# A three-block transformer stack on one core: the distance table's load moved behind a meeting, first latent parts in front of it, attention heads in another order

## The chip, the cores and the metric

The kernel runs on one NeuronCore of one Trainium2 chip. A core has five engines that run side by side and meet only at semaphores: TensorE (PE in the profile; PEld is its weight load), VectorE (DVE), ScalarE (ACT), GpSimd (POOL) and SyncE (SP), which here only starts transfers. The metric is the time of one execution on the device in microseconds (us), lower is better. All arithmetic is float32; TensorE multiplies float32 values that have been split into a rounded high part and a remainder (low part).

## The reference

One token sequence of 512 tokens with 1024 features goes through a first block, and then through a second block with two layers. The change touches only the mixing part of those two layers:

```python
for l in range(DEPTH_2):                                   # two layers
    x = x + 0.5 * swiglu(rms_norm(x, ffn1_norm[l]), ...)
    h = rms_norm(x, mix_norm[l])
    pa, pb, pc, pd = jnp.split(h @ w_in[l], IN_SPLITS, axis=-1)
    ya = neighbourhood_mixer(pa, ...)      # 4 near heads: q reads 8 rows x 32 columns of keys, plus a bias
    yb = mla_mixer(pb, ...)                # 4 latent heads: 96 wide, 512 keys
    yc = diff_mixer(pc, ..., t5_bias, ...) # 4 differential heads: softmax of 2 maps each, bias by distance
    yd = gqa_mixer(pd, ...)                # 4 shared heads: 2 key heads, 512 keys
    x = x + jnp.concatenate([ya, yb, yc, yd], axis=-1) @ w_out[l]
    x = x + 0.5 * swiglu(rms_norm(x, ffn2_norm[l]), ...)
    x = rms_norm(x, final_norm[l])
```

The four mixers are independent of each other, so their heads can be computed in any order. Each head is softmax(q k + bias) v; the bias of the differential heads is a table by distance (t5_bias), that of the near heads a table by offset.

## The kernel before, in words

The program is a row of stages. Between stages stands a meeting (`handover`, L393): every engine drains its queue, says so on a semaphore, and waits until the others have said it. GpSimd's drain is L421. SyncE waits for the same four semaphores before the first transfers of the next stage.

Each of the two layers has a stage `mixer_inputs` and then a stage `mixers`. `mixer_inputs` multiplies the normalized input by 22 units of weights; at its end GpSimd waits for the last unit, and issues the transfer of the distance table (L2618, 1792 KB) into `hlo`, a buffer that TensorE reads until that last unit. Then comes the meeting.

`mixers` runs `attention` (L956) on 20 groups of 4 steps, 80 steps in all, one step for 128 queries of one head (or of one of the two maps of a differential head). Before the change the groups are: latent heads (steps 0 to 15), near heads (16 to 31), shared heads (32 to 47), differential heads (48 to 79). A step t is:

- TensorE, L985: scores(t), three products of 512 columns (latent, shared), three of 256 (near), or one of 512 (differential), into one of four banks
- VectorE, L1071 or, with a bias, L1078: the row minimum `low` (scores are kept with their sign turned)
- ScalarE, L1032: the exponential, `prob`
- TensorE, L993: four (near: two) transposes of `prob`; ScalarE, L1039: copy to `probT`
- TensorE, L1004: product with the values `vB`, `vA`, `vD`, `vC` (latent, near, shared, differential)

TensorE's queue holds scores(t+4), the transposes of t, the values of t-2, in this order for t = 0, 1, 2 and so on; each waits in order. Scores are four steps ahead and have four banks, so scores(t+4) waits until the exponential (with a bias: the minimum) of step t is done.

The query side lives in two slots of four tiles in `hhi`, used in turn (`user` lists the first step of each user of a slot, `ends` the first step after it). VectorE fills them: `splits` (L2106) puts pieces of work at given steps t of its queue: `parts` writes high parts (a cast, L2111) and low parts (a subtraction, L2115). A piece that overwrites a slot first waits for `qk_done`, the count of score steps done, of the slot's user two before. Latent heads 0 and 1 are written at t = -1, the start of the stage. Key parts that several heads share go to `parted`, 8 tiles.

Near and shared queries fill 64 of 128 partitions. The other 64 are zeroed by GpSimd (L2081), once for each slot, after it has added the near heads' bias and mask (L2065, 12 additions, `nabias`), which in turn wait for SyncE's 9 loads (L2051, L2054).

The differential heads' slots are not written by VectorE. SyncE copies them from `parted` with 16 transfers of 64 KB for a head (L2101, L2104; "stack load" below), four such loads for u = 10 to 13, and before each it waits for `parted`, and for `qk_done` to reach `ends[u - 2]`.

Of the kernel before, what the change touches and what calls it, by code (L numbers as in the profile page):

```python
# [24 lines left out]
P = 128  # L25
# [2002 lines left out]
def mixers(k, mem, l, near, latent, diff, shared, parted, lam, ytok):  # L2028
# [11 lines left out]
    diff_parts = [apart[0:2] + apart[6:8], apart[2:6]]  # L2040
    user = list(range(0, 32, 4)) + list(range(32, 80, 8))
# [18 lines left out]
    def _(pool):  # L2060
        pool.wait_ge(*k.t5_landed.all())
        pool.wait_ge(*loaded)
        for h in range(4):
            for o in range(3):
                nc.gpsimd.tensor_tensor(bias[:, h, o, :].rearrange("p (r j) -> p r j", j=32),  # L2065
                                        wide[:, h, :, 16 - 8 * o:48 - 8 * o],
                                        mask[:, o, :].rearrange("p (r j) -> p r j", j=32), ALU.add)\
                    .then_inc(*k.na_ready.up())

# [14 lines left out]
    ready = {user[h]: [k.latent_split.at(h + 1)] for h in range(4)}  # L2084
    for v in range(4):
        ready[user[4 + v]] = [k.keys_split.at(1 + v // 2), zeroed[v % 2], k.padded.at(v + 1)]
    for v in range(2):
        ready[user[8 + v]] = [k.keys_split.at(3), k.padded.at(5 + v)]
# [19 lines left out]
    def splits(dve, t):  # L2108
# [27 lines left out]
        if t == -1:  # L2136
            latent_head(0)
# [4 lines left out]
        if t in (5, 9):  # L2142
            c = (t - 5) // 4
            parts([(kA[:, c, :], *near_keys[c])], k.keys_split)
        if t in (8, 12, 16, 20):
            h = (t - 8) // 4
            dve.wait_ge(*k.qk_done.at(ends[2 + h]))
            r = 64 * (h % 2)
            parts([(qA[r:r + 64, h // 2, :], slot[h % 2][0][r:r + 64], slot[h % 2][1][r:r + 64])], k.padded)
        if t == 13:  # L2150
            parts([(kD[:, :], *shared_keys)], k.keys_split)
        if t in (24, 28):
            v = (t - 24) // 4
            dve.wait_ge(*k.qk_done.at(ends[6 + v]))
# [3 lines left out]
        if t in (30, 48):  # L2158
            c = 0 if t == 30 else 1
# [7 lines left out]
    for h in range(4):  # L2167
# [4 lines left out]
                           out=ytok[:, :, GW + h * 64:GW + h * 64 + 64], add=False, factor=None))  # L2172
    for h in range(4):
# [9 lines left out]
    for v in range(2):  # L2183
        for j in range(2):
            h = 2 * v + j
            groups.append(dict(steps=[dict(pairs=three(slice(u * P, (u + 1) * P), *slot[v][2 * j:2 * j + 2], shared_keys),
                                           width=T, bias=None, values=[vD[:, t, v, :] for t in range(TB)])
                                      for u in range(TB)],
                               out=ytok[:, :, 3 * GW + h * 64:3 * GW + h * 64 + 64], add=False, factor=None))
# [10 lines left out]
    sums = {45: (1, bias[:, :, 0, :]), 47: (0, bias[:, :, 1, :]), 61: (6, bias[:, :, 2, :]), 68: (2, head(0)),  # L2200
            76: (3, head(1)), 82: (4, head(2))}

    def squares(act, t):
        if t in (44, 46, 60):
            i = (44, 46, 60).index(t)
            at, done = ((GW, 4), (0, 8), (3 * GW, 12))[i]
            act.wait_ge(*k.o_read.at(done))
            if i == 0:
                act.wait_ge(*k.low_done.at(32))
# [12 lines left out]
    attention(k, groups, mem, bias_ready=(4 * TB, na_ready), ready=ready, splits=splits, on_act=squares)  # L2222
# [33 lines left out]
def mixer_inputs(k, w, l, near, latent, diff, shared, lat_parts, lam, gain, sb):  # L2256
# [245 lines left out]
    def _(dve):  # L2502
# [7 lines left out]
        for s in range(2 * UNITS + 1):  # L2510
# [66 lines left out]
            if s in parts:  # L2577
# [5 lines left out]
                    .then_inc(*k.rn_ready.up())  # L2583
            if s == 40:
# [11 lines left out]
    def _(pool):  # L2596
# [16 lines left out]
        for r in range(8, 11):  # L2613
            cosine(r)
        t5 = k.hlo[:, 0:7, :].rearrange("p c t -> p (c t)").rearrange("p (h t) -> p h t", h=4)
        pool.wait_ge(k.units_done.sem, n0 + UNITS)
        pool.wait_ge(k.tables_out, 32)
        pool.dma_start(t5, bass.AP(k.t5_dram.tensor, 0, [[1, P], [1024, 4], [1, 896]]).bitcast(F32R))\  # L2618
            .then_inc(*k.t5_landed.up(by=16))
# [176 lines left out]
def build(nc, w, consts, out):  # L2796

    with ExitStack() as ctx:
# [22 lines left out]
        k.into_landed = signal("into_landed")  # L2821
# [115 lines left out]
```

## Time and profile before

| what | value |
|---|---|
| median of 3 runs | 3440.15 us (3438.2 to 3444.74) |
| profiled execution, its own time | 3431.85 us |
| its span | 3430.1 us |
| granted TensorE clock over the span, of 1 | 0.968 |
| PE, PEld, DVE, ACT, POOL busy | 97%, 78%, 51%, 38%, 6% |
| chain that ended last, by engine | PE 89%, DVE 6%, issue 2%, ACT 2% |
| `mixers` of the first layer, meeting to the last product with values | 1695.02 to 1861.89 us |
| `mixers` of the second layer, the same | 2832.95 to 2993.18 us |

A row of the timeline has: start in us, duration in us, engine, line, operation, out<-in, count, and in brackets the idle time of the engine just before it and what ended it. A row of the windows has: the stretch, its length, busy time of each engine with the number of instructions, the granted TensorE clock (1.00 is 2.4 GHz, 0.50 is 1.2 GHz), the mean busy share of the DMA engines and GB/s. Matmuls overlap, so the time that one takes from the next is read from start to start.

### The profile page before, as it was taken

The numbers are of one execution on the slowest core, as the hardware profiler recorded it, in microseconds if no ns is written. First come the engines' busy times: TensorE is split into PE (matmuls) and PEld (weight loads), VectorE is DVE, ScalarE is ACT, GpSimd is POOL, SyncE is SP. The second block draws the span as 40 slices with busy tenths as digits, with TensorE's granted clock in tenths as the row PEclk, the third lists the DMA queues.
The fourth block names the chain that finished last, engine by engine and source line by source line (L and its number), as shares of the span: only waits on it lengthen the run. The fifth ranks groups of instructions, "written<-read, shape, count | busy, mean of one in ns | idle before, by whom it ended". The sixth has DMA issues, their size and how long they took to land.

```text
span 3430.1 us, 41354 instructions
## 1 busy us (share of the span) xinstructions
PE 3320.0 (97%) x15399; PEld 2659.7 (78%) x15399; DVE 1764.3 (51%) x2614; ACT 1299.0 (38%) x1849; POOL 213.8 (6%) x234
## 2 busy tenths in 40 slices
PE   8979998999999999999899999999999998999998
PEld 6667876888888888875598888878887567878887
DVE  7354487445553455335646555445553565555532
ACT  4326655233332333223246333333322324643332
POOL 1001100000000000010200100010000011010000
PEclk9969999999999999999979999999999997999999
DMA  5310022333333333332202333333333321223332
GB/s 126 92 49 4 1 68 80 96 94 94 95 95 96 97 94 92 99 93 68 70 13 66 90 96 96 94 92 98 98 97 88 85 60 27 69 86 98 97 91 63
DMA packets 518249, 275.12 MB, mean 80 GB/s; under 512 B 39523, under 2 KB 510407, under 8 KB 517986
## 3 DMA queue, kind: packets, MB, share of 16 engines
q1 hardware_dynamic: 513154, 262.77, 27.6%
q0 software_dynamic: 3600, 9.85, 0.9%
q8 instruction: 89, 1.46, 0.2%
q10 hardware_dynamic: 1360, 0.66, 0.1%
q14 instruction: 46, 0.38, 0.0%
HBM read 262.70 MB, written 2.14 MB: 77 GB/s over the span
## 4 chain that ended last, share of the span: by engine, by line
PE 89%; DVE 6%; issue 2%; ACT 2%; POOLq 0%; POOL 0%; DMA 0%; DVEq 0%; ACTq 0%
PE bank L375 24%; PE bank L376 24%; PE bank L377 24%; PE bank L1004 5%; PE bank L985 5%; PE bank L993 3%; PE bank L2389 1%; DVE wlo L351 1%; PE bank L1688 1%; PE bank L2372 1%; POOLq L421 0%; PE bank L2359 0%; DVE xc L1894 0%; DVE q L932 0%; PE bank L690 0%
## 5 line engine op out<-in xcount | busy, mean ns | idle before, releaser
L375 PE MATMUL bank<-hhi,whi 128*128 128x512 f32 (+1 forms) x2504 | 992.6, 396 | 7.4 <-DVE wlo L351 5.1
L376 PE MATMUL bank<-hhi,wlo 128*128 128x512 f32 (+1 forms) x2504 | 977.2, 390 | 0.0
L377 PE MATMUL bank<-hlo,whi 128*128 128x512 f32 (+1 forms) x2504 | 977.1, 390 | 0.0
L351 DVE TENSOR_TENSOR wlo<-raw,whi 128x1024 fp32r<-128x1024 f32 x485 | 608.6, 1257 | 587.2 <-ACT whi L344 578.3
L344 ACT CAST whi<-raw 128x1024 fp32r<-128x1024 f32 x485 | 505.1, 1046 | 408.6 <-PE bank L377 394.9
L375 PEld LDWEIGHTS bank<-hhi,whi 128*128 128x128 f32 (+1 forms) x2504 | 470.4, 188 | 149.0 <-issue 45.1
L377 PEld LDWEIGHTS bank<-hlo,whi 128*128 128x128 f32 (+1 forms) x2504 | 470.4, 188 | 100.2
L376 PEld LDWEIGHTS bank<-hhi,wlo 128*128 128x128 f32 (+1 forms) x2504 | 470.8, 188 | 99.0 <-issue 3.4
L375 PE MATMUL bank<-uhi,whi 128*128 128x512 f32 x880 | 348.7, 396 | 0.0
L376 PE MATMUL bank<-uhi,wlo 128*128 128x512 f32 x880 | 348.2, 396 | 0.0
L377 PE MATMUL bank<-ulo,whi 128*128 128x512 f32 x880 | 348.2, 396 | 0.0
L594 ACT CAST uhi<-gate 128x512 f32 x110 | 68.2, 620 | 597.1 <-DVE gate L618 597.1
L611 DVE TENSOR_TENSOR up<-bank,rinv 128x512 f32<-128x512 f32 x110 | 76.0, 691 | 288.1 <-PE bank L377 288.1
L1039 ACT COPY probT<-bank 128x512 f32<-128x512 f32 (+3 forms) x288 | 140.5, 488 | 148.1 <-PE bank L993 147.0
L377 PEld LDWEIGHTS bank<-ulo,whi 128*128 128x128 f32 x880 | 165.4, 188 | 39.9
L375 PEld LDWEIGHTS bank<-uhi,whi 128*128 128x128 f32 x880 | 165.4, 188 | 39.8
L376 PEld LDWEIGHTS bank<-uhi,wlo 128*128 128x128 f32 x880 | 165.4, 188 | 39.4
L463 POOL TENSOR_TENSOR sq<-sq 128x512 f32<-128x512 f32 x49 | 63.8, 1302 | 1825.6 <-ACT sq L481 1825.6
L993 PEld LDWEIGHTS bank<-ident,prob 128*128 128x128 f32 x896 | 120.0, 149 | 46.8 <-issue 24.6
L993 PE MATMUL bank<-ident,prob 128*128 128x128 f32 x896 | 154.6, 286 | 0.9 <-ACT prob L1032 0.6
L621 DVE TENSOR_TENSOR ulo<-gate,uhi 128x512 f32 x110 | 76.2, 693 | 99.5 <-ACT uhi L594 99.5
L985 PE MATMUL bank<-kT,q 128*128 128x128 f32 (+3 forms) x256 | 98.1, 469 | 5.3 <-POOLq L421 5.3
(443 smaller groups left out, 3651.8 us busy)
## 6 DMA issues: line engine op xcount, KB each, us to landing
raw<-in_ffn_w_gate SPq DMA_DIRECT2D x88, 512.0 KB, 3.8
raw<-in_ffn_w_up SPq DMA_DIRECT2D x88, 512.0 KB, 3.7
raw<-in_w_in SPq DMA_DIRECT2D x78, 512.0 KB, 3.8
raw<-in_ffn_w_down SPq DMA_DIRECT2D x64, 512.0 KB, 4.0
raw<-in_w_out SPq DMA_DIRECT2D x24, 512.0 KB, 4.1
raw<-in_ffn_w_down SPq DMA_DIRECT2D x32, 384.0 KB, 3.4
raw<-in_w_gate SPq DMA_DIRECT2D x22, 512.0 KB, 3.9
raw<-in_w_up SPq DMA_DIRECT2D x22, 512.0 KB, 3.7
```

The lines of the kernel that those rows point to most:

```text
L344: k.nc.scalar.copy(k.whi[:, slot, :], k.raw[:, slot, :]).then_inc(k.hi_split.sem, 1)
L351: k.nc.vector.tensor_tensor(k.wlo[:, slot, :], k.raw[:, slot, :], k.whi[:, slot, :].bitcast(F32), ALU.subtract)\
L375: mm(out, whi, hi(kc), start=start and i == 0, stop=False)
L376: mm(out, wlo, hi(kc), start=False, stop=False)
L377: last = mm(out, whi, lo(kc), start=False, stop=stop and i == kcs - 1)
L594: nc.scalar.copy(uhi[:, bass.ds(i * 2 + e, 1), :], gate[:, e:e + 1, :])\
L611: nc.vector.tensor_tensor(up[:, e, :], bank[u + 1][:, :], k.rinv[:, :], ALU.mult)\
L621: nc.vector.tensor_tensor(ulo[:, bass.ds(i * 2 + e, 1), :], gate[:, e:e + 1, :], uhi[:, bass.ds(i * 2 + e, 1), :].bitcast(F32), ALU.subtract)\
L985: last = nc.tensor.matmul(score(t), q, key, start=i == 0, stop=i == len(pairs) - 1)
L993: last = nc.tensor.transpose(k.bank[4 + t % 2][:, b * P:b * P + P], prob[:, t % 2, b * P:b * P + P], k.ident[:, :])
L1004: last = nc.tensor.matmul(mixed(g)[:, e, :], probT[:, t % 3, b * P:b * P + P], v, start=b == 0, stop=b == len(values) - 1)
L1039: nc.scalar.copy(probT[:, v % 3, 0:width[v]], k.bank[4 + v % 2][:, 0:width[v]])\
```

## The change

Three things, in each of the two layers.

1. The load of the distance table leaves the end of `mixer_inputs`, and is the first thing that GpSimd does in `mixers`, behind the meeting. GpSimd waits for its landing after the 12 additions, no longer before them.
2. The parts of latent head 0 leave t = -1 of `attention`, and are computed by VectorE at the end of `mixer_inputs`, in front of the meeting.
3. The order of heads is latent (steps 0 to 15), shared (16 to 31), near (32 to 47), differential (48 to 79). `user`, the places in `parted`, the steps of the pieces in `splits` and of the sums of squares follow.

```diff
-    diff_parts = [apart[0:2] + apart[6:8], apart[2:6]]
-    user = list(range(0, 32, 4)) + list(range(32, 80, 8))
+    diff_parts = [apart[4:8], apart[0:4]]
+    user = [0, 4, 8, 12, 16, 24, 32, 36, 40, 44, 48, 56, 64, 72]
...
     def _(pool):
-        pool.wait_ge(*k.t5_landed.all())
+        distances = k.hlo[:, 0:7, :].rearrange("p c t -> p (c t)").rearrange("p (h t) -> p h t", h=4)
+        pool.wait_ge(k.tables_out, 32)
+        pool.dma_start(distances, bass.AP(k.t5_dram.tensor, 0, [[1, P], [1024, 4], [1, 896]]).bitcast(F32R))\
+            .then_inc(*k.t5_landed.up(by=16))
         pool.wait_ge(*loaded)
...
                     .then_inc(*k.na_ready.up())
+        pool.wait_ge(*k.t5_landed.all())
...
-    ready = {user[h]: [k.latent_split.at(h + 1)] for h in range(4)}
+    ready = {user[h]: [k.latent_split.at(h)] for h in range(1, 4)}
+    for v in range(2):
+        ready[user[4 + v]] = [k.keys_split.at(1), zeroed[v], k.padded.at(v + 1)]
     for v in range(4):
-        ready[user[4 + v]] = [k.keys_split.at(1 + v // 2), zeroed[v % 2], k.padded.at(v + 1)]
-    for v in range(2):
-        ready[user[8 + v]] = [k.keys_split.at(3), k.padded.at(5 + v)]
+        ready[user[6 + v]] = [k.keys_split.at(2 + v // 2), k.padded.at(3 + v)]
...
         if t == -1:
-            latent_head(0)
             latent_head(1)
...
-        if t in (5, 9):
-            c = (t - 5) // 4
-            parts([(kA[:, c, :], *near_keys[c])], k.keys_split)
-        if t in (8, 12, 16, 20):
-            h = (t - 8) // 4
-            dve.wait_ge(*k.qk_done.at(ends[2 + h]))
-            r = 64 * (h % 2)
-            parts([(qA[r:r + 64, h // 2, :], slot[h % 2][0][r:r + 64], slot[h % 2][1][r:r + 64])], k.padded)
-        if t == 13:
+        if t == 5:
             parts([(kD[:, :], *shared_keys)], k.keys_split)
-        if t in (24, 28):
-            v = (t - 24) // 4
-            dve.wait_ge(*k.qk_done.at(ends[6 + v]))
+        if t in (8, 12):
+            v = (t - 8) // 4
+            dve.wait_ge(*k.qk_done.at(ends[2 + v]))
             r = 64 * v
             parts([(qD[r:r + 64, j, :], slot[v][2 * j][r:r + 64], slot[v][2 * j + 1][r:r + 64]) for j in range(2)],
                   k.padded)
-        if t in (30, 48):
-            c = 0 if t == 30 else 1
+        if t in (14, 18):
+            c = (t - 14) // 4
+            parts([(kA[:, c, :], *near_keys[c])], k.keys_split)
+        if t in (20, 28, 32, 36):
+            h = (20, 28, 32, 36).index(t)
+            dve.wait_ge(*k.qk_done.at(ends[4 + h]))
+            r = 64 * (h % 2)
+            parts([(qA[r:r + 64, h // 2, :], slot[h % 2][0][r:r + 64], slot[h % 2][1][r:r + 64])], k.padded)
+        if t in (34, 48):
+            c = 0 if t == 34 else 1
...
-        if t in (44, 46, 60):
+        if t in (50, 52, 60):
...
+            if s == 2 * UNITS:
+                for x, to in ((qB, 0), (kB, 2)):
+                    nc.vector.tensor_copy(k.hhi[0:MD, to, :], x[0:MD, 0, :]).then_inc(*k.latent_hi.up())
+                for i, (x, to) in enumerate(((qB, 0), (kB, 2))):
+                    dve.wait_ge(*k.latent_hi.at(i + 1))
+                    nc.vector.tensor_tensor(k.hhi[0:MD, to + 1, :], x[0:MD, 0, :], k.hhi[0:MD, to, :].bitcast(F32),
+                                            ALU.subtract)
...
-        t5 = k.hlo[:, 0:7, :].rearrange("p c t -> p (c t)").rearrange("p (h t) -> p h t", h=4)
-        pool.wait_ge(k.units_done.sem, n0 + UNITS)
-        pool.wait_ge(k.tables_out, 32)
-        pool.dma_start(t5, bass.AP(k.t5_dram.tensor, 0, [[1, P], [1024, 4], [1, 896]]).bitcast(F32R))\
-            .then_inc(*k.t5_landed.up(by=16))
```

On GpSimd, around the meeting of the first layer (L419 ends the old stage, L2059 begins the new one; `ytok` holds the near table while it is added):

```order
-L2618 DMA hlo<-t_by_distance 128x4x896 [waits tables_out,units_done]
...
 L419 UNCONDITIONAL_BRANCH
 L2059 UNCONDITIONAL_BRANCH [waits dve_finished,act_finished,pe_finished]
-L2065 TENSOR_TENSOR nabias<-ytok 128x256 [waits offsets_landed,t5_landed]
-L2065 TENSOR_TENSOR nabias<-ytok 128x256 x11
-L2073 UNCONDITIONAL_BRANCH
-L2081 MEMSET hhi 64x2048 [waits qk_done,na_ready]
-L2081 MEMSET hhi 64x2048 [waits slot_zeroed,qk_done]
+L2063 DMA hlo<-t_by_distance 128x4x896 [waits tables_out]
+L2068 TENSOR_TENSOR nabias<-ytok 128x256 [waits offsets_landed]
+L2068 TENSOR_TENSOR nabias<-ytok 128x256 x11
+L2077 UNCONDITIONAL_BRANCH [waits t5_landed]
+L2085 MEMSET hhi 64x2048 [waits qk_done,na_ready]
+L2085 MEMSET hhi 64x2048 [waits slot_zeroed,qk_done]
```

The load has moved past the meeting, and the wait for it past the 12 additions; the two memsets still stand behind the additions.

On VectorE, the start of `mixers` before (L1044 is its first instruction behind the meeting):

```order
1013 L2593 TENSOR_SCALAR lam<-lam 128x1 [waits lam_dot]
1014 L413 UNCONDITIONAL_BRANCH
1015 L1044 UNCONDITIONAL_BRANCH [waits pool_finished,act_finished,pe_finished]
1016 L2111 CAST hhi<-qB 96x512
1017 L2111 CAST hhi<-kB 96x512
1018 L2115 TENSOR_TENSOR hhi<-qB,hhi 96x512 [waits part_hi]
1019 L2115 TENSOR_TENSOR hhi<-kB,hhi 96x512
1020 L2111 CAST hhi<-qB 96x512
```

and now, where after latent head 3 and the shared keys the shared queries `qD` of step 8 follow:

```order
1013 L2603 TENSOR_SCALAR lam<-lam 128x1 [waits lam_dot]
1014 L2589 CAST hhi<-qB 96x512
1015 L2589 CAST hhi<-kB 96x512
1016 L2592 TENSOR_TENSOR hhi<-qB,hhi 96x512 [waits latent_hi]
1017 L2592 TENSOR_TENSOR hhi<-kB,hhi 96x512 [waits latent_hi]
1018 L413 UNCONDITIONAL_BRANCH
1019 L1044 UNCONDITIONAL_BRANCH [waits pool_finished,act_finished,pe_finished]
1020 L2115 CAST hhi<-qB 96x512
...
1036 L2115 CAST parted<-kD 128x512
1037 L2119 TENSOR_TENSOR parted<-kD,parted 128x512 [waits part_hi]
1038 L1071 TENSOR_REDUCE low<-bank 128x1 [waits qk_done,exp_done] x3
1039 L2115 CAST hhi<-qD 64x512 [waits qk_done]
```

Four instructions have moved in front of the meeting, and the queries behind step 8 are the shared heads' four instructions instead of the near heads' two.

On TensorE, the last of near head 3 and the first differential step now (`stacked0` is the landing of the stack load into slot 0):

```order
5010 L985 MATMUL bank<-parted,hhi 128x256 [waits low_done]
5011 L985 MATMUL bank<-parted,hhi 128x256 x2
5012 L993 MATMUL bank<-ident,prob 128x128 [waits pt_copied,exp_done]
5013 L993 MATMUL bank<-ident,prob 128x128
5014 L1004 MATMUL bank<-vA,probT 128x65 [waits pt_copied]
5015 L1004 MATMUL bank<-vA,probT 128x65
5016 L985 MATMUL bank<-hhi 128x512 [waits stacked0,low_done]
5017 L993 MATMUL bank<-ident,prob 128x128 [waits pt_copied,exp_done]
```

Before, the steps ahead of that wait were those of the last shared head:

```order
5011 L985 MATMUL bank<-parted,hhi 128x512 [waits exp_done]
5012 L985 MATMUL bank<-parted,hhi 128x512 x2
5013 L993 MATMUL bank<-ident,prob 128x128 [waits pt_copied,exp_done]
5014 L993 MATMUL bank<-ident,prob 128x128 x3
5015 L1004 MATMUL bank<-vD,probT 128x65 [waits pt_copied]
5016 L1004 MATMUL bank<-vD,probT 128x65 x3
5017 L985 MATMUL bank<-hhi 128x512 [waits stacked0,exp_done]
```

The first differential scores now stand behind narrow near steps, where wide shared ones stood; by `ends[8]`, the stack load of slot 0 waits for `qk_done` = 44 (`user[9]`), where it waited for 40.

## Rows read from the trace of the kernel before

**Rows 1.** Windows: `mixers` of the first layer, from the meeting to the last values.
```profile
1695.02:1861.89 166.87, 157.62 (x1040) 145.29 (x1040) 90.08 (x221) 93.72 (x169) 16.30 (x17) 0.85 0.20 44
```

**Rows 2.** Timeline and chain that ended last: the meeting of the first layer.
```profile
1687.42 0.80 POOL L2618 DMA_DIRECT2D hlo<-t_by_distance  x1 [13.84 <-PE bank L377]
1687.40 7.62 POOLq L421
1688.68 0.15 DVE L2593 TENSOR_SCALAR lam<-lam 128x1 f32<-128x1 f32 x1
1695.35 0.42 DVE L2111 CAST hhi<-qB 96x512 fp32r<-96x512 f32 x1 [6.52 <-POOLq L421]
1697.49 5.84 PE L985 MATMUL bank<-hhi 96*128 96x512 f32 x15 [8.80 <-DVE hhi L2115]
```

**Rows 3.** Windows of TensorE alone: its stretches at either clock.
```profile
1697.49:1702.07 4.58, 4.58 (x11) 0.50 0.93 175
1715.76:1760.14 44.38, 44.38 (x193) 0.50 0.00 1
1760.14:1861.90 101.76, 98.44 (x775) 1.00 0.24 58
2852.40:2883.06 30.66, 30.57 (x122) 0.50 0.00 1
2883.06:2993.20 110.14, 106.80 (x849) 1.00 0.22 54
```

**Rows 4.** Timeline: GpSimd's additions, latent head 3's parts, TensorE's gap (second layer last).
```profile
1707.75 10.22 POOL L2065 TENSOR_TENSOR nabias<-ytok 128x256 f32<-128x256 f32 x12 [19.52 <-DMA ytok<-na_by_offset]
1709.23 0.91 DVE L2111 CAST hhi<-qB 96x512 fp32r<-96x512 f32 x1 [2.68 <-PE bank L985]
1712.07 1.20 DVE L2115 TENSOR_TENSOR hhi<-kB,hhi 96x512 fp32r<-96x512 f32 x1
1714.71 0.96 PE L985 MATMUL bank<-hhi 96*128 96x512 f32 x3 [2.19 <-ACT prob L1032]
2852.49 1.65 PE L985 MATMUL bank<-hhi 96*128 96x512 f32 x3 [1.74 <-ACT prob L1032]
```

**Rows 5.** Timeline: scores of neighbouring steps: latent, shared, near, differential, a pair each.
```profile
1721.52 1.63 PE L985 MATMUL bank<-hhi 96*128 96x512 f32 x3
1725.36 1.63 PE L985 MATMUL bank<-hhi 96*128 96x512 f32 x3
...
1787.85 0.94 PE L985 MATMUL bank<-parted,hhi 128*128 128x512 f32 x3
1789.88 0.95 PE L985 MATMUL bank<-parted,hhi 128*128 128x512 f32 x3
...
1760.58 0.61 PE L985 MATMUL bank<-parted,hhi 128*128 128x256 f32 x3
1761.61 0.61 PE L985 MATMUL bank<-parted,hhi 128*128 128x256 f32 x3
...
1816.88 0.49 PE L985 MATMUL bank<-hhi 128*128 128x512 f32 x1
1818.45 0.48 PE L985 MATMUL bank<-hhi 128*128 128x512 f32 x1
```

**Rows 6.** Windows: while only the distance table was moving.
```profile
1690.00:1694.00 4.00, 0.00 (x0) 0.00 (x0) 0.00 (x0) 0.00 (x0) 0.00 (x0) 0.73 1.08 384
```

**Rows 7.** SyncE's timeline: first load and last load of the first layer's stack loads.
```profile
1784.82 2.52 SPq L2101 DMA_DIRECT2D hhi<-parted  x4
...
1793.24 2.49 SPq L2104 DMA_DIRECT2D hhi<-parted  x4
...
1828.41 2.41 SPq L2101 DMA_DIRECT2D hhi<-parted  x4
...
1835.93 2.49 SPq L2104 DMA_DIRECT2D hhi<-parted  x4
```

**Rows 8.** By tile `parted`: from issue to landing, least, median, most.
```profile
DMA to landing us min/median/max: 1.9/2.0/3.3
```

More of the change, by code:

```diff
@@ L2172, in mixers @@
                            out=ytok[:, :, GW + h * 64:GW + h * 64 + 64], add=False, factor=None))
+    for v in range(2):
+        for j in range(2):
+            h = 2 * v + j
+            groups.append(dict(steps=[dict(pairs=three(slice(u * P, (u + 1) * P), *slot[v][2 * j:2 * j + 2], shared_keys),
+                                           width=T, bias=None, values=[vD[:, t, v, :] for t in range(TB)])
+                                      for u in range(TB)],
+                               out=ytok[:, :, 3 * GW + h * 64:3 * GW + h * 64 + 64], add=False, factor=None))
     for h in range(4):
@@ L2182, in mixers @@
         groups.append(dict(steps=heads, out=ytok[:, :, h * 64:h * 64 + 64], add=False, factor=None))
[L2183 to L2189, printed above, removed]
     for h in range(4):
@@ L2199, in mixers @@
     head = lambda h: bias[:, :, 0, h * HD:(h + 1) * HD]
-    sums = {45: (1, bias[:, :, 0, :]), 47: (0, bias[:, :, 1, :]), 61: (6, bias[:, :, 2, :]), 68: (2, head(0)),
+    sums = {51: (1, bias[:, :, 0, :]), 53: (6, bias[:, :, 1, :]), 61: (0, bias[:, :, 2, :]), 68: (2, head(0)),
             76: (3, head(1)), 82: (4, head(2))}
     def squares(act, t):
-        if t in (44, 46, 60):
-            i = (44, 46, 60).index(t)
-            at, done = ((GW, 4), (0, 8), (3 * GW, 12))[i]
+        if t in (50, 52, 60):
+            i = (50, 52, 60).index(t)
+            at, done = ((GW, 4), (3 * GW, 8), (0, 12))[i]
             act.wait_ge(*k.o_read.at(done))
             if i == 0:
-                act.wait_ge(*k.low_done.at(32))
+                act.wait_ge(*k.low_done.at(48))
             nc.scalar.activation(bias[:, :, i, :], ytok[:, :, at:at + GW], ACT.Square).then_inc(*k.y_sq.up())
@@ L2220, in squares @@
                                      bias=k.eps[:, 0:1]).then_inc(*k.y_root.up())
-    attention(k, groups, mem, bias_ready=(4 * TB, na_ready), ready=ready, splits=splits, on_act=squares)
+    attention(k, groups, mem, bias_ready=(8 * TB, na_ready), ready=ready, splits=splits, on_act=squares)
     @k.block.vector
@@ L2821, in build @@
         k.into_landed = signal("into_landed")
+        k.latent_hi = signal("latent_hi")
         k.x_odd, k.vt_copied, k.t5_landed = signal("x_odd"), signal("vt_copied"), signal("t5_landed")
```

## The prediction

> **What bounds the kernel now.** The page first: TensorE is busy 97% of the span and 89% of the chain that ended last, so only what makes TensorE wait, or run at the lower clock, can be won. The change lies in the two `mixers` stages, so the windows of these come next: in the first layer 166.9 us with TensorE busy for 157.6 of them, at a mean granted clock of 0.85 [rows 1]. So some 9 us of the stage are gaps, and more is lost to the clock. The timeline of the meeting shows the largest gap. GpSimd issues the distance table's load at 1687.42, and its drain ends 7.62 us later, about when the load has landed; VectorE waits 6.52 us for it, then splits latent head 0 for 2.14 us, and TensorE starts at 1697.49 after 8.80 us without work [rows 2]. The windows by clock come third. TensorE ran at 0.50 (1.2 GHz) right after the meeting, again from 1715.76 to 1760.14, and in the second layer from 2852.40 to 2883.06; the rest ran at 1.00 (2.4 GHz) [rows 3]. The timeline ahead of the two later falls shows why: VectorE is at latent head 3's parts, and TensorE has nothing for 2.19 us in the first layer, 1.74 in the second; during or just behind these the clock falls [rows 4]. It came back only after 44 and 31 us, though TensorE was busy throughout.
>
> What a step costs TensorE, start to start: latent at the lower clock 3.84 us; shared at the higher 2.03, near 1.03, differential 1.57 [rows 5]. A latent step has the same instructions as a shared one, so 2.03 for it too. The full clock would nearly halve both low stretches.
>
> **The start of the stage.** With the table's load behind the meeting, GpSimd drains at once. VectorE's last instruction in front of it ends at 1688.83; the four instructions for head 0 take 2.14 us there as they did behind it, to 1690.97 [rows 2]. Some 0.25 us for the meeting itself (the first cast started 0.33 after the drain's end) makes TensorE start at 1691.2 and not 1697.49: -6.3 us for each layer, -12.6 in all. What is late next: the parts of head 1, 2.1 us again, which hold the first minimum as before, so the pipeline starts shifted by the same amount. TensorE's gap at the meeting falls from 8.8 to about 2.5 us. The table's own landing has until step 48 to come.
>
> **The first seam: GpSimd's additions against VectorE's parts.** While GpSimd adds, head 3's parts take 4.04 us (1709.23 to 1713.27) and not the 2.1 that they take alone; a cast is 0.91 and not 0.42 [rows 4, 2]. TensorE has work for 3.3 us from 1709.23 (its gap of 2.19 ends at 1714.71), and minimum and exponential take 1.44 behind the parts: 4.04 + 1.44 - 3.3 is the gap. Alone, the parts would leave 0.3. GpSimd began 12.7 us behind the meeting. Now the table's 1792 KB share the DMA engines with the near tables; alone they moved at 384 GB/s [rows 6], so at most 4.7 us later: 17.4. Head 3's parts now come at about 10 to 12 us, in front of the additions. But the four instructions of step 8 (shared queries) stand at 18 to 20 us, right on them: 4.0 us and not 2.1. The steps around are of the same kind, so the gap is 2.2 us, as before but four steps later. So I expect the clock to fall again, at step 13. If the additions began 3 us later the gap would be gone. I take a low stretch of 14 us for each layer (before it was 31 and 44, never rose among latent steps and rose among those of the heads behind them, in the second layer at the first ones; now only three latent steps, 11.5 us, are left behind the gap). Lost before: half of 44.4 and 30.7, 37.5 us; lost now: half of 28, 14 us. Term: -23.5, between -37.5 (no fall) and +31 (low until the near heads at step 32: 19 steps that lose 1.81 each, 34 us a layer). The value is nearest to the row of the second layer, where the rise came with the first step of another kind.
>
> The Trainium skill has a rule for this seam (SBUF — State Buffer, "Who interferes with whom"): a VectorE instruction with two SBUF inputs or in a two-port mode and a GpSimd one exclude each other, and the later blocks until the earlier ends. By that rule each of the four would wait for up to one addition of 0.85 us (10.22 / 12), 3.4 in all; the rows have 1.9 in all, so the trace agrees that they hinder each other, and the price by rows is the lower. By the rule's 3.4 the gap would be 3.7 us, and the sum 3 us higher over both layers.
>
> GpSimd's memset for the first shared slot needs additions (10.2) and memset (1.9): 17.4 + 12.1 = 29.5 us, when step 16's scores are due at about 29 to 31. Cost 0 to 0.5; I take 0.
>
> **The second seam: the first stack load.** 16 transfers leave SyncE from 1784.82 to 1795.73, 10.9 us; the fastest of the first layer's four, 1828.41 to 1838.42, 10.0 us; landing 2.0 more [rows 7, 8]. So 12.0 to 12.9 us from the slot being free to step 48's scores. Before, it started when the scores of step 39 were done, and 8 shared steps of 2.03 (16.2 us) covered it. Now the slot's last user is near head 2: it starts after step 43, and ahead of step 48's scores TensorE has only four near steps (4.1) and one set of transposes and values (0.6): 4.7 us. It then waits 12.7 - 4.7 = 8.0 us, in each layer: +16, between +14.6 and +16.4. Nothing else can run there: transposes stand behind the scores in TensorE's queue. ScalarE's two squares of steps 50 and 52 and VectorE's sums, formerly over steps 44 to 47, fall just behind it, where the others have caught up, so cost nothing.
>
> Eight idle us are more than the gaps after which the clock fell, so it falls. How long it stays low among differential heads no row shows. Low, a differential step would be about 1.57 x 3.84 / 2.03 = 3.0 us, 1.4 more. The bounds are 0 and all 32 steps (+45 for a layer). I take some 8 steps (24 us at the low clock would lose 11; I shade to 12 us, since the first steps behind the wait have their work ready and TensorE has no gap): +6 for each, +12 in all. It is nearest to the restart behind the meeting, which was back at 1.00 after 4.6 us [rows 3], and far from the two long ones; that is the weakest term. At the low clock the second stack load (12 us) hides behind 8 steps; at the high one it would stick out by 1.7 us.
>
> **The near heads.** TensorE's gaps at the higher clock, 101.76 - 98.44 and 110.14 - 106.80, 3.3 us in each layer [rows 3], come from VectorE's pieces of work between near steps (near, shared and differential parts in one run of 16 short steps). Now half of these pieces stand in the wide latent and shared steps, where 3.3 us of TensorE's work cover 1.1 for a piece of two instructions and 1.4 for minimum and exponential: -2.5 for each, -5.
>
> **Sum.** -12.6 - 23.5 + 16 + 12 - 5 = -13. The restart behind the meeting is shorter and less likely at the low clock: -2.3 at best, I take -2. So -15 against the profiled execution's own 3431.85 (span 3430.1, 1.75 around it): 3417. The three runs lie 6 to 13 us above that execution. Its second layer had 14 us less at the low clock than its first, which is worth 7; runs with both stretches long are the usual ones, and the new order has less to lose there. So against the median of 3440.15 I take -20: 3420.
>
> **Rivals.**
>
> - *The clock holds, or is back at once.* If the additions miss step 8's parts and the fall at step 48 lasts only as after the meeting: -12.6 - 37.5 + 16 + 4 + 3.4 (second stack load in sight) - 5 - 2 = -34, some 3400 to 3406. For it: the additions' start is within 3 us of missing. Against: 8 us of idling are certain by the rows.
> - *Slower: the differential heads run at the low clock.* Place: step 48, where the stack load leaves TensorE idle. Price: 45 us a layer instead of 6. In both layers: -15 + 78 = +63, 3500; in one, or half the way in both: +20 to +25, 3460. It decides once the low stretch behind step 48 lasts over 27 us a layer. For it: before, a busy TensorE stayed low for 31 and 44 us [rows 3], and no row shows the clock rising among differential steps. Against: the clock did rise in the narrow steps of the near heads.
> - *Nothing left over.* The stall of 8 us and long low stretches (about 25 us at each of the two places) eat the start's gain: 3434 to 3446. What I call the low stretches' lengths is the only thing to change.
> - *The start is not won.* GpSimd's drain could be slow for another reason than the load. Then TensorE starts about 2 us earlier only, +8: 3428. Against: its 7.62 us go with the load's time. Small.
>
> **Chances.** Forecast (two short low stretches, or one long) 0.42; clock holds 0.18; slower 0.24, of which one layer 0.14; nothing left 0.13; start not won 0.03. A difference under 0.2% (7 us) can't be told from none. Faster: 0.42 + 0.18 + 0.03, less 0.03 for the forecast's upper edge: 0.60. Same: 0.13 and that edge: 0.15. Slower: 0.25. The forecast's own range is 3408 to 3431. The range for 8 in 10 leaves out the best of the clock's case and the two-layer loss: 3398 to 3456.
>
> **What would show it.** Timeline: TensorE starts 2 to 3 us after its last product in front of the meeting, with no 7.6 us drain. A gap of some 2 us before the scores of step 13 with VectorE's `qD` parts at twice their time, next to GpSimd's additions. A gap of 7 to 9 us in front of the first differential scores, put down to the DMA into `hhi`. Windows by clock: 0.50 behind each. I'd be wrong if that gap is under 4 us (the stack load is quicker, or near steps slower), or if the clock behind it is low for over 27 us or for none.

## The result, and the profile after

| what | before | after |
|---|---|---|
| median, in one comparison | 3438.2 us (5 runs) | 3416.69 us (5 runs, 3409.7 to 3420.75) |
| ratio of the two, 95% interval | | 0.994 (0.9924 to 0.9956) |
| profiled execution, its own time | 3431.85 us | 3416.69 us |
| last product in front of the meeting to last product with values, layer one / two | 173.2 / 166.6 us | 158.8 / 160.8 us |

The change makes the kernel 21.5 us, or 0.6%, faster; 3420 had been predicted, in a range of 3398 to 3456. Of the two traces the stages account for 14.4 and 5.8 us, 20.2 in all. TensorE comes 4.06 us later to the first meeting in the profiled execution of after (1692.75 where it was 1688.69), in a part that the change doesn't touch: in the first block its granted clock was 0.50 for 17.1 us from 242.06 on, where it had been for 6.8 us from 241.2 on. The other parts outside the two stages lose 1 us more, so the own times differ by only 15.2.

The timeline of the meeting in the kernel after, against [rows 2]:

```profile
1692.81 0.41 DVE L2589 CAST hhi<-qB 96x512 fp32r<-96x512 f32 x1
1694.08 0.68 DVE L2592 TENSOR_TENSOR hhi<-kB,hhi 96x512 fp32r<-96x512 f32 x1
1695.12 0.72 PE L985 MATMUL bank<-hhi 96*128 96x512 f32 x2 [2.37 <-DVEq L415]
1695.53 0.80 POOL L2063 DMA_DIRECT2D hlo<-t_by_distance  x1 [17.88 <-DVEq L415]
2819.19 1.22 PE L985 MATMUL bank<-hhi 96*128 96x512 f32 x2 [2.38 <-DVEq L415]
```

TensorE's gap of 8.80 is 2.37 and 2.38. The drain of 7.62 us is gone, and what is waited for now is VectorE's.

The timeline of the first seam after, against [rows 4]:

```profile
1712.34 9.54 POOL L2068 TENSOR_TENSOR nabias<-ytok 128x256 f32<-128x256 f32 x12 [16.00 <-DMA ytok<-na_by_offset]
1714.87 1.42 DVE L2115 CAST hhi<-qD 64x512 fp32r<-64x512 f32 x2 [3.03 <-PE bank L985]
1716.33 2.24 DVE L2119 TENSOR_TENSOR hhi<-qD,hhi 64x512 fp32r<-64x512 f32 x2
1719.26 0.69 ACT L1032 ACTIVATE prob<-bank,low 128x512 f32<-128x512 f32 x1 [3.31 <-DVE low L1071]
1720.00 1.65 PE L985 MATMUL bank<-hhi 96*128 96x512 f32 x3 [1.87 <-ACT prob L1032]
2845.35 0.97 PE L985 MATMUL bank<-hhi 96*128 96x512 f32 x3 [2.26 <-ACT prob L1032]
```

The additions begin 17.2 us behind the restart (TensorE's first product behind the meeting, at 1695.12), on top of the four pieces of `qD`. Those take 3.7 us (1714.87 to 1718.57), the minimum and the exponential follow late, and TensorE has nothing for 1.87 us. The windows of TensorE alone, against [rows 3]:

```profile
1696.14:1699.55 3.41, 3.41 (x9) 0.50 1.00 212
1719.90:1733.60 13.70, 13.60 (x51) 0.50 0.00 0
1733.70:1788.30 54.60, 52.07 (x411) 1.00 0.05 13
1792.85:1798.40 5.55, 5.55 (x22) 0.50 0.38 87
1798.60:1851.50 52.90, 51.63 (x427) 1.00 0.33 80
2846.40:2859.90 13.50, 13.50 (x58) 0.50 0.00 0
2919.22:2924.80 5.58, 5.58 (x22) 0.50 0.43 101
```

The long low stretches of 44.38 and 30.66 us have become 13.7 and 13.5, and two short ones are new. These lie behind the second seam; TensorE's timeline there, then SyncE's:

```profile
1785.27 0.56 PE L1004 MATMUL bank<-vA,probT 128*128 128x65 f32 x4
1792.85 0.77 PE L985 MATMUL bank<-hhi 128*128 128x512 f32 x1 [7.02 <-DMA hhi<-parted]
...
2919.22 0.76 PE L985 MATMUL bank<-hhi 128*128 128x512 f32 x1 [8.16 <-DMA hhi<-parted]
```

```profile
1781.20 2.52 SPq L2105 DMA_DIRECT2D hhi<-parted  x4
...
1788.82 2.49 SPq L2108 DMA_DIRECT2D hhi<-parted  x4
```

The stack load starts at 1781.20, and its landing lets TensorE go on 11.65 us later; TensorE has been out of work since 1785.83.

### The profile page after: what moved, and what is told of

Its sections match the earlier page's. It is cut to its first block, busy times and chain, and to the rows that moved or that the text cites. A ratio compares the mean times of both kernels' runs of the same rounds, so it can differ in the third digit from the quotient of the medians.

```text
span 3414.9 us, 41348 instructions
## 1 busy us (share of the span) xinstructions
PE 3306.4 (97%) x15399; PEld 2645.2 (77%) x15399; DVE 1762.5 (52%) x2614; ACT 1298.9 (38%) x1849; POOL 211.8 (6%) x234
## 3 DMA queue, kind: packets, MB, share of 16 engines
q8 instruction: 89, 1.46, 0.2%
## 4 chain that ended last, share of the span: by engine, by line
PE 90%; DVE 6%; ACT 2%; issue 1%; SPq 1%; DMA 0%; DVEq 0%; POOL 0%; ACTq 0%; POOLq 0%; PEldq 0%
PE bank L375 24%; PE bank L377 24%; PE bank L376 24%; PE bank L1004 5%; PE bank L985 5%; PE bank L993 3%; PE bank L2392 1%; DVE wlo L351 1%; PE bank L2375 1%; PE bank L1688 1%; PE bank L2362 1%; DVE xc L1894 0%; DVE q L932 0%; PE bank L690 0%; PE bank L1707 0%
```

## The experiments

Each difference between two kernels is taken from their ratios to the kernel before (in brackets behind each time, with the 95% interval), in us of 3440. A ratio's own interval is about 0.2% either way, so 7 us, and kernels that were compared together share the runs of the kernel before.

**The two halves of the change alone.** `start_only` is the kernel before, with the first two of the three things:

```diff
-        pool.wait_ge(*k.t5_landed.all())
...
+        pool.dma_start(distances, bass.AP(k.t5_dram.tensor, 0, [[1, P], [1024, 4], [1, 896]]).bitcast(F32R))\
...
+        pool.wait_ge(*k.t5_landed.all())
...
-            latent_head(0)
...
+            if s == 2 * UNITS:
+                for x, to in ((qB, 0), (kB, 2)):
```

> The kernel before, with only the start of the change: the distance table's load behind the meeting, latent head 0's parts in front of it; heads in the old order. Theory (each part of the change does what its rows say, and the parts add up): TensorE starts 6.4 us earlier behind both meetings, -12.8. GpSimd's additions move from 12.7 to about 17.4 us behind the meeting, past latent head 3's parts and onto the near heads' pieces, which have two instructions and not four; so the gap at step 7 goes, any later gap is under 1.5 us, and the long low stretches (half of 44 and 31 us lost) shrink or go: 3390 to 3412. Rival 1 (the start gains, but the clock falls as before, since the additions are not what makes the gap): 3425. Rival 2 (the drain is slow for another reason than the load): TensorE's first gap stays over 6 us, 3434.

3383.54 us (0.9853, 0.9831 to 0.9875): 51 us faster than before, better than the theory's 3390 to 3412, and 30 us faster than the whole change. Its timeline, and one window of the first layer:

```profile
1702.45 0.42 DVE L2115 CAST hhi<-qB 96x512 fp32r<-96x512 f32 x1 [2.68 <-PE bank L985]
1708.48 9.62 POOL L2068 TENSOR_TENSOR nabias<-ytok 128x256 f32<-128x256 f32 x12 [16.02 <-DMA ytok<-na_by_offset]
1711.02 0.54 DVE L2115 CAST hhi<-qA 64x512 fp32r<-64x512 f32 x1 [3.03 <-PE bank L985]
1711.59 1.11 DVE L2119 TENSOR_TENSOR hhi<-qA,hhi 64x512 fp32r<-64x512 f32 x1
```

```profile
1695.00:1833.10 138.10, 132.92 (x1031) 1.00 0.29 62
```

Latent head 3's parts begin at 1702.45, 6.0 us ahead of the additions; in [rows 4] they began 1.5 us behind their start. The additions now fall on pieces of two instructions (1.7 us for the first), which fit beside a latent step, and the clock stays at 1.00 from the end of the restart's low stretch (1695.46) to the end of the stage. 12.8 us of start and 37.5 us of clock make 50.3, and the two stages are 50.9 us shorter by the traces.

`order_only` has the third thing alone:

```diff
-        distances = k.hlo[:, 0:7, :].rearrange("p c t -> p (c t)").rearrange("p (h t) -> p h t", h=4)
...
+        pool.wait_ge(*k.t5_landed.all())
         pool.wait_ge(*loaded)
...
         if t == -1:
+            latent_head(0)
```

> The changed kernel with the old start: the table's load in front of the meeting and latent head 0's parts behind it, heads in the new order. Theory: 8.8 us without work at both meetings as before; the additions meet latent head 3's parts as before, gap of about 2 us at step 7, and a low stretch of 20 to 44 us in a layer; a wait of 7 to 8 us in front of step 48 with a low stretch of 5 to 7 us behind it, +21 for both layers. Against before: +21, less up to 5 for near steps and up to 15 for shorter low stretches: 3442 to 3458, slower. If the parts add up, this difference and that of the start alone make -21 together. Rival (the order itself is the gain: wide shared steps bring the clock back sooner than near ones): 3425 to 3437.

3441.28 us (1.0016, 1.0005 to 1.0028), 5.5 us slower than before, just under the theory's 3442 to 3458. The wait at step 48 is there (7.05 and 8.04 us), and so is the fall at latent head 3:

```profile
1720.90:1748.20 27.30, 27.30 (x111) 0.51 0.00 1
2857.30:2884.60 27.30, 27.30 (x110) 0.51 0.00 1
```

27.3 us twice, where the kernel before has 44.38 and 30.66: 10 us won. In this order the clock comes back at 1748.50 and 2885.14, 3.1 and 2.3 us behind the first shared scores (1745.44, 2882.83). So the order alone costs 15.1 for the two waits and 5.5 for the clock behind them, and wins some 4 at the near heads and 10.2 here: about +6, where the stages' traces have +4.2. The two halves do not add up: 5.5 and -50.6 make -45, where the two together give -20.6.

**The start taken apart.** In the kernel before, the table's load alone:

```diff
-        pool.wait_ge(k.units_done.sem, n0 + UNITS)
-        pool.wait_ge(k.tables_out, 32)
-        pool.dma_start(t5, bass.AP(k.t5_dram.tensor, 0, [[1, P], [1024, 4], [1, 896]]).bitcast(F32R))\
```

> The kernel before, with the distance table's load behind the meeting alone; latent head 0's parts stay behind it, old order. Theory: VectorE has only 0.2 us from its last work to the meeting, so the 2.1 us of parts lie behind TensorE's last product in either place, and moving them in front gains only 0.2 to 0.4 us as soon as the drain is short. TensorE's gap 2.6 to 2.9 us and not 8.8; GpSimd's additions at 17.4 us as in the kernel with the start alone, so no gap at step 7 and no long low stretch: 3384 to 3389. Rival (the parts' place matters by itself, 2.1 us a layer and the distance to the additions): gap of 4.5 us, 3390 to 3400.

and head 0's parts alone:

```diff
-            latent_head(0)
...
+                for x, to in ((qB, 0), (kB, 2)):
+                    nc.vector.tensor_copy(k.hhi[0:MD, to, :], x[0:MD, 0, :]).then_inc(*k.latent_hi.up())
```

> The kernel before, with latent head 0's parts in front of the meeting alone; the table's load stays in front of it too, old order. Theory: GpSimd's drain of 7.6 us stays, TensorE starts 2.1 to 2.4 us earlier, -4.5 for both layers. Latent head 3's parts come 2.1 us earlier against the additions (start 12.7 us behind the meeting) and still meet most of them: gap of 1.0 to 1.9 us at step 7. If the clock falls as before: 3428 to 3433; if such a smaller gap is no longer enough: 3390 to 3400, which would say that the collision is a matter of 1 or 2 us. I expect the first, 60 to 40.

`load_only`: 3401.73 us (0.9908, 0.9889 to 0.9927), 13 us over the expectation's upper edge. `parts_only`: 3426.45 (0.9968, 0.9953 to 0.9984), 2 us below the first of its two cases, in 12 runs from 3410.75 to 3432.95. The one traced took 3431.51, and what the fastest did differently is not shown. In it TensorE's gap at the meeting is 6.46 us, the fall at step 7 is there (gap of 1.73), the low stretches are 44.3 and 27.2. So the drain was the load's, and the load's place is the larger part. But the parts in front are worth more than their 0.7 us of the gap at the meeting (3.09 in `load_only`, 2.37 in `start_only`). The timeline of `load_only`, first layer, then second:

```profile
1711.05 8.65 POOL L2068 TENSOR_TENSOR nabias<-ytok 128x256 f32<-128x256 f32 x12 [15.36 <-DMA ytok<-na_by_offset]
1716.39 3.59 DVE L2115 CAST hhi<-qA 64x512 fp32r<-64x512 f32 x1 [3.03 <-PE bank L985]
1722.14 0.97 PE L985 MATMUL bank<-hhi 96*128 96x512 f32 x3 [2.48 <-ACT prob L1032]
...
2839.38 2.10 DVE L2115 CAST hhi<-qA 64x512 fp32r<-64x512 f32 x1 [2.13 <-PE bank L985]
2839.40 1.80 POOL L2085 MEMSET hhi<- 64x2048 f32 x1 [2.05 <-PE bank L985]
2843.76 1.01 PE L985 MATMUL bank<-parted,hhi 128*128 128x256 f32 x3 [1.46 <-ACT prob L1032]
```

VectorE's work runs 2.8 us later against the additions than in `start_only` (their start lies 14.4 us behind TensorE's, and not 17.2). One cast took 3.59 us and not 0.42: it ended 0.28 us behind the last of the additions (1719.98 and 1719.70). The gap of 2.48 us behind it brought no fall. In the second layer a cast met the memset, took 2.10 us and again ended 0.28 us behind it, and behind the gap of 1.46 the clock fell for 10.2 us. My expectation had only counted the gap at the meeting; the phase between GpSimd and VectorE carried the rest.

**The second seam alone.** In the kernel after, near heads 2 and 3 use the third and fourth tile of a slot, which no near head uses otherwise; so the first half of a stack load need only wait for near head 0 or 1:

```diff
-            parts([(qA[r:r + 64, h // 2, :], slot[h % 2][0][r:r + 64], slot[h % 2][1][r:r + 64])], k.padded)
+            a = 2 * (h // 2)
+            parts([(qA[r:r + 64, h // 2, :], slot[h % 2][a][r:r + 64], slot[h % 2][a + 1][r:r + 64])], k.padded)
...
-            sp.wait_ge(*k.qk_done.at(ends[u - 2]))
...
             for m in range(2):
+                sp.wait_ge(*k.qk_done.at(ends[u - 2 if m or u >= 12 else u - 4]))
...
+                k.slot_loads[u % 2 + 2 * m] += 8 * 16
+                ready[user[u] + 4 * m] = [(k.stacked[u % 2 + 2 * m], k.slot_loads[u % 2 + 2 * m])]
```

> The changed kernel, with near heads 2 and 3 in the third and fourth tile of their slot, and each of the first two stack loads in two halves: the first, of tiles one and two, may start when near head 0 (or 1) is done, 8 steps sooner than now, and only the second waits for near head 2 (or 3). Theory: the wait at step 48 (7.0 and 8.2 us) goes, and with it the low stretch behind it (TensorE at work for 5.7 us a layer at half the clock, 2.8 lost): -15 -6 = -21 against the changed kernel, 3396. Rival 1 (the first differential steps are low in any case, their minimum with a bias being slower): only -15, 3402. Rival 2 (the second half is late in its turn, a new wait at step 52): -5 to -10.

3390.07 us (0.9868, 0.9846 to 0.9889): 25 us below the kernel after, where 21 was expected. (The scores of near heads 2 and 3 read the new tiles too, and each half has a semaphore of its own; these lines are left out above.) SyncE's timeline and TensorE's:

```profile
1776.23 2.53 SPq L2105 DMA_DIRECT2D hhi<-parted  x4
1778.80 2.49 SPq L2108 DMA_DIRECT2D hhi<-parted  x4
1782.63 2.41 SPq L2105 DMA_DIRECT2D hhi<-parted  x4
```

```profile
1786.11 0.60 PE L985 MATMUL bank<-parted,hhi 128*128 128x256 f32 x3
...
1787.13 0.48 PE L985 MATMUL bank<-hhi 128*128 128x512 f32 x1
```

The first half starts 10.9 us ahead of need and is issued in 5.1, and the first differential scores follow the last near ones at once, at the full clock. So the differential heads can run at 1.00 from the first, and the low 5.6 us of the kernel after come from the wait. No wait at step 52 took its place.

**The first seam alone.** In the kernel after, GpSimd's work goes to where VectorE has little:

```diff
+            pool.wait_ge(*k.padded.at(s + 1))
...
         pool.wait_ge(*loaded)
+        pool.wait_ge(*k.keys_split.at(2))
         for h in range(4):
...
-            pool.wait_ge(*k.qk_done.at(ends[2 + s]))
...
+        if t == 24:
+            dve.wait_ge(*na_ready)
```

> The changed kernel, with GpSimd's 12 additions behind the key parts of step 14, and its two memsets in front of them, each behind the shared query parts (steps 8 and 12), so that nothing of GpSimd stands beside the four-instruction pieces. Theory (the additions double step 8's pieces, the gap that follows brings the clock down): step 8's four parts take 2.1 us and not 3.6, the gap of 1.87 and 2.26 us at step 13 goes, and the low stretches of 13.8 and 13.7 us: -14 from the clock and -2 to -4 from the gaps, 3398 to 3402. Rival (the shared pieces are long enough by themselves, or the clock falls for another reason): no change, 3414 to 3418. Rival 2 (the additions, now beside the parts of steps 18 and 20, make the same gap there): the fall only moves, 3412 to 3420.

3397.0 us (0.9888, 0.9869 to 0.9907), 18 us below the kernel after and 1 below the theory's 3398 to 3402. Timeline and window:

```profile
1715.37 0.75 DVE L2116 CAST hhi<-qD 64x512 fp32r<-64x512 f32 x2 [3.03 <-PE bank L985]
1716.15 1.29 DVE L2120 TENSOR_TENSOR hhi<-qD,hhi 64x512 fp32r<-64x512 f32 x2
1717.50 1.80 POOL L2075 MEMSET hhi<- 64x2048 f32 x1 [20.67 <-DVE hhi L2120]
```

```profile
1700.00:1781.00 81.00, 76.49 (x581) 1.00 0.21 40
```

The same four instructions take 2.1 us without GpSimd beside them and 3.7 with it. There is no gap at step 13 and no fall, in either layer. The edit moves the memsets too, but in the kernel after the first of these starts at 1721.94, behind the gap. So it is the additions that make the gap, which the prediction had read from a coincidence alone.

**Both seams.** 

> The changed kernel with both mendings: GpSimd's additions behind the key parts of step 14 with the memsets ahead of them (which alone went from 3416.7 to 3397.0), and the first two stack loads in halves (which alone went to 3390.1). Theory (the two seams are apart from each other, one at step 13, one at step 48): the gains add up, 19.7 + 26.6 = 46, 3370, TensorE without a gap over 1.3 us between the restart and the last values, the clock at 1.00 throughout but for the restart; 1 to 3 us per layer may be left at step 52 or 56 by the stack loads, since all steps ahead of them run at the full clock. Rival (the heads' order costs something besides its two seams, so the kernel with the start alone, 3383.5, stays ahead): 3384 to 3395.

3377.3 us (0.9836, 0.9819 to 0.9854), 56 us below before and 36 below the kernel after, 7 above the theory's 3370. The two gains alone would make 43; whether they overlap by a few us, or the intervals make the difference, is not shown. The stage takes 139.0 us from restart to last value in the first layer, at 1.00 throughout but for the restart:

```profile
1700.00:1830.10 130.10, 127.81 (x1012) 1.00 0.25 55
```

It was run once more beside the kernel with the start alone:

> The changed kernel with both mendings once more, now on one chip with the kernel that has the start alone. Theory (the new order, once its two seams are closed, is worth what was put down to the near heads' gaps, some 2.5 us a layer): in the two traces so far the stage from restart to last value took 139.0 and 139.6 us here and 141.9 and 142.2 with the start alone, so 5 to 6 us faster: 3376 to 3379. Rival (the 6 us between them were two chips' difference): within 2 us of each other.

> The kernel before with the start alone once more, beside the changed kernel with both mendings. Theory: 3382 to 3385, 5 to 6 us above it. Rival: no difference over 2 us.

3377.02 us (3374.98 to 3382.26; 0.9823, 0.9804 to 0.9843) against 3388.59 (3384.3 to 3394.88; 0.9858, 0.9838 to 0.9879). No run of the one is above any of the other, though the intervals of the ratios touch; `start_again` was 4 us above the upper end of what was expected. The windows of the first layer's stage, `both_again` and then `start_again`:

```profile
1695.80:1830.40 134.60, 131.07 (x1029) 1.00 0.29 63
...
1701.60:1838.30 136.70, 131.90 (x1028) 1.00 0.28 61
```

From restart to last value the stages take 139.0 and 139.6 us against 141.4 and 141.6, so the order with its two seams closed is worth some 4.5 us in these two traces (5.4 in those of `both` and `start_only`). Much of what lies between the two times is not the order's: of the 9.4 us between the two profiled executions 5.5 are there before the first meeting, where the kernels are alike.

**Why the low stretches are long.** The latent heads' scores read 96 of 128 rows. In the kernel before, read over all 128:

```diff
-        qhi, qlo, khi, klo = (x[0:MD] for x in slot[h % 2])
+        qhi, qlo, khi, klo = (x[0:P] for x in slot[h % 2])
```

> The kernel before, with the latent heads' scores over 128 rows and not 96: 32 rows of leftovers of the stage ahead come into each product, so its latent heads compute something else; columns, number and order of all instructions stay. Why: in the five long low stretches seen so far the clock came back 2.2 to 4.1 us behind the first scores that are not a latent head's. Theory (it is the latent products, 96 of 128 rows, that don't bring the clock back): the gap of 1.7 to 2.2 us at step 7 stays and the clock falls there, but the low stretches shorten from 44.4 and 30.7 us to under 14 each: -9 to -32, 3403 to 3426. If it holds throughout, 3398. Rival (the length has to do with the other engines' rhythm in latent steps, or with time alone): stretches of 30 to 44 us, 3435 as before.

A sentence of it is wrong. In the kernel before, the first scores that are not a latent head's are these. In the first layer the clock came back at 1760.14, 19.4 us behind them and not 2 to 4; in the second layer it was 3.7:

```profile
1740.72 0.99 PE L985 MATMUL bank<-parted,hhi 128*128 128x256 f32 x3
...
2879.39 0.99 PE L985 MATMUL bank<-parted,hhi 128*128 128x256 f32 x3
```

`wide_latent` took 3407.37 us (0.9921, 0.9904 to 0.9938), 27 below the kernel before and inside the theory's 3403 to 3426. Windows, first layer and second:

```profile
1720.60:1724.00 3.40, 3.40 (x16) 0.51 0.00 0
1724.30:1850.00 125.70, 120.11 (x950) 1.00 0.20 47
...
2861.00:2871.00 10.00, 10.00 (x48) 0.50 0.01 2
```

The gaps are as large as ever (2.12 and 2.29), the clock falls, and is back after 3.4 us in both layers, not after 44.4 and 30.7. The edit changes the number of rows and, with it, the values in them and behind them; which of these counts is not shown. Nor is it the 96 rows by themselves: right behind each meeting scores of 96 rows follow one another without transposes or values between them, and there the clock came back after 4.6 us of work in the kernel before (6.7 in its second layer). In the second layer of `wide_latent` it fell again among the near heads, behind a gap of 1.45, and stayed low for 10 us. The same edit in the kernel after:

> The changed kernel, with the latent heads' scores over 128 rows and not 96 (32 rows of leftovers of the stage ahead come into each product, so its latent heads compute something else). Theory (the clock comes back in latent products too, once these fill all rows): the gap of about 2 us at step 13 stays, the low stretch behind it is 3 to 7 us and not 13.7, the one behind step 48 stays at 10: -7 to -10, 3406 to 3410. Rival (in the kernel before it was the place in the stage that made the difference, 128 rows by themselves do nothing): 3414 to 3418.

3408.16 us (0.991, 0.9893 to 0.9927), 10 us below the kernel after, as the theory had it. Behind the gap of 1.76 in the first layer the low stretch is 3.4 us; in the second a gap of 2.26 brought none. Step 16 now shows a gap of 2.04, which the lower clock had covered before: the `qD` pieces of step 12 meet a memset (two casts take 2.44 us, where they take 0.76 in `late_adds`).

## Why the prediction was right, point by point

| term | predicted | measured, both layers |
|---|---|---|
| start | -12.6 | -12.8: gap 8.80 to 2.37 and 2.38 |
| low stretches of the first seam | -23.5 | -23.9: half of 75.0 was lost, half of 27.2 is |
| wait at step 48 | +16 | +15.2: 7.02 and 8.16 |
| low clock behind it | +12 | +5.6: half of 5.55 and 5.58 |
| near heads' gaps | -5 | -4.3: 1.3 and 1.0 us left of 3.3 each |
| restart | -2 | -0.6: 3.4 us low and not 4.6, second layer 6.8 and 6.7 |
| sum | -15 | -21, where the stages' traces differ by 20.2 |

- **The first seam** went as written: additions 17.2 us behind the restart (17.4 behind the meeting estimated), on step 8's pieces, gaps of 1.87 and 2.26 us, a fall in front of the last latent steps. The reason given for 14 us, that the clock does not rise among latent steps but among those behind, held: it rose 2.1 and 4.1 us behind the first shared scores (1731.54, 2855.99), and `wide_latent` ties the length to what the latent scores read. What was not seen is whose gain it is. The start alone brings 37.5 us here, since the additions then meet only short pieces, and the order gives 14 of them back. The sum treats the change as a whole, so it could be right without that: it has -12.6 for the start and books the rest under the order's seam, while the start alone is worth 50.
- **By the Trainium skill** (SBUF — State Buffer, "Who interferes with whom"), the later of two such instructions waits until the earlier ends. The trace agrees that they hinder each other: step 8's four took 1.6 us more than alone, near the rows' 1.9 and below the 3.4 that the rule would give. But the cast of `load_only` lost 3.2 us at once, more than four additions of 0.72 (8.65 / 12), and it ended with the whole run of additions, so one addition is no bound for a single wait. That pieces beside a memset suffer too (2.10 us and not 0.42) fits the page's remark on copies in a two-port mode.
- **The second seam**: the load took 11.65 us where 12.0 to 12.9 stood in the sum, and the cover was 4.6 (1781.20 to 1785.83). The mechanism and the price were right, and `halves` shows it by taking the wait away.
- **"I take some 8 steps"**, the weakest term by its own words, was the step that was mis-sized. The clock was low for the first four differential steps. It had fallen at 1788.3, while TensorE was idle, so 4.5 of the 10.1 us at the low clock cost nothing. 2.8 us a layer and not 6. That is like the restart, which the text itself named as the nearest row. The slower rival (over 27 us a layer, chance 0.24) had little to it: 5.6. Its evidence, the 31 and 44 us, came from steps with 96 rows and from narrow ones.
- **The sum against the median**: -20 was said and -21.5 measured. In the traces -15 came out as -15.2 because the clock term's 6.4 too much met 5 us that were lost outside the two stages, nearly 4 of them in the first block, where the clock was low for longer. That the own times agree to 0.2 us is luck; that the stage terms do, apart from one, is not. The further 5 us between -15 and -20 were put down to the second layer's shorter low stretch as unusual, and the runs do not bear that out: it is the shorter one in `parts_only` too (27.2 and 44.3). What they show is that TensorE's part ahead of the first meeting, the same in all kernels, varies: its last product ends at 1688.7 to 1689.1 in four traces, that of the kernel before among them, and at 1692.8 to 1695.0 in nine. So that -20 is close to -21.5 is partly luck as well.
- The rival of a start that is not won is refuted by the gap of 2.37 us at the meeting; that nothing is left over, by the short stretches; that the clock holds at the first seam, with the wait at step 48 still there, is what `late_adds` is: 3397, where 3400 to 3406 stood for it.

## What to carry to other kernels

Price a moved transfer or instruction by what the rest then meets: here 7.5 us of shift between GpSimd's additions and VectorE's pieces (from 1.5 us ahead of head 3's parts to 6.0 behind them) was worth 37.5 us, three times the 12.8 that the move itself won. Where two changes are made at once, read the seam of each as if the other were not made; one may spend what the other wins, as the order did with 30 of the start's 50 us. And ask of every reused buffer what covers its next load in the new order: when wide steps become narrow ones, the cover goes, and splitting the load by what is needed first, into tiles that come free earlier, gives it back.

## What the runs showed of the hardware

- How long TensorE stayed at 1.2 GHz depended on what it multiplied. Among latent steps (f32 scores over 96 rows, transposes and value products between them) it never rose behind a fall: 27.3 us twice in `order_only`, with TensorE busy for all of it. With scores over 128 rows in the same places, and other values, it was back in 3.4. Where scores of 96 rows followed one another alone, behind the meetings, it was back after 3.4 to 6.8 us of work. It came back 1.2 to 4.1 us behind the first shared scores (128 rows, 512 columns) in both layers of the kernel after, `order_only` and `halves`; with near scores (256 columns) it took 3.7 and 3.8 us in one layer of the kernel before and of `parts_only`, and 19.4 and 19.5 in the other.
- A gap of 2 us lets the clock fall but need not. Among latent heads and at step 16 there were 17 gaps of 1.73 to 2.48 us in these kernels. The clock fell behind 13 of them, and held behind 2.26, 2.04 and 2.06 (`wide_after`) and 2.48 (`load_only`). Among near heads it fell behind two of four gaps of 1.45 or 1.46 (`load_only`, `wide_latent`), and in no run behind the gap of 1.2 to 1.3 us that follows most restarts.
- One VectorE cast of 64x512 took from 0.42 us (alone) through 0.54 and 2.10 to 3.59, by what GpSimd did beside it; the two long ones ended 0.28 us behind GpSimd's run of additions and its memset.
